# Rounding and halving the memory's weight slabs one place earlier in the queues of ScalarE and VectorE

## The chip, the cores and the metric

One core of one Trainium2 chip runs the whole program. The metric is the device time of one execution in microseconds (us); the kernel before was run three times and the median is compared.

## What is computed

The reference is two transformer blocks, one after the other, on 512 tokens of width 1024. The change touches the second block only, which has two layers. In each layer the memory's 256 tokens are normalised and projected to keys and values, the layer's own mixing output is projected and added to x, and x attends to the memory:

```python
mix = jnp.concatenate([out_a, out_b, out_c], axis=-1) @ w_mix_out[l]
x = x + rms_norm_2(mix, mix_post_g[l])
h = rms_norm_2(x, mem_pre_g[l])
mem_n = rms_norm_2(mem, mem_kv_g[l])
...
q = (h @ w_q).reshape(b, s, X_HEADS, X_HEAD_DIM)
kv = (mem_n @ w_kv).reshape(b, m, 2, X_HEADS, X_HEAD_DIM)
k, v = kv[:, :, 0], kv[:, :, 1]
sc = jnp.einsum('bqhd,bkhd->bhqk', q, k).astype(jnp.float32) * (X_HEAD_DIM ** -0.5)
p = jax.nn.softmax(sc, axis=-1).astype(v.dtype)
o = jnp.einsum('bhqk,bkhd->bqhd', p, v).reshape(b, s, D_MODEL)
return o @ w_o
```

## The kernel before

All weights come as one stream of slabs of 16 blocks of 128 x 128 numbers (1 MB). A slab passes four hands. SyncE loads it into one of four places of `ring` (`Stream.feed`, L372 issues). ScalarE rounds it to the short float form into one of three places of `ring_hi` (`Stream.round`, L264). VectorE subtracts this from the slab and writes the rest, its lower half, back over it, `ring_lo` (`Stream.halve`, L271). TensorE multiplies in three parts, upper by upper, upper by lower, lower by upper (`Stream.mm`, L322). TensorE reports each slab that it has begun (`slab_begun`). SyncE may load slab g once slab g-3 is begun, and ScalarE may round slab g once slab g-2 is begun, since `ring_hi` holds three.

The order on each engine is written out by hand. `ws.round_to(act, s, ...)` in ScalarE's code and `ws.halve_to(dve, s, ...)` in VectorE's put the roundings and halvings of all slabs up to s at that place of the queue. An engine works its queue in order, so whatever stands ahead of a rounding delays it.

Two stages matter. `mix_and_memory` (L1891) first projects the mixing output. Then TensorE makes eight key tiles, `key_tile(0)` to `key_tile(7)`, of 24 matmuls each, two tiles to a slab, and from two more slabs half of the values, 24 matmuls to a slab. Beside this, for each of eight column tiles of x, ScalarE evicts a key tile (`key_out`, L2009), rounds the new h (`round_h`, L2019) and squares x (L2020), while VectorE scales the projection (`scaled`, L2075), splits h (`split_h`, L2086) and adds to x (`new_x`, L2081). `round_h(n)` waits for `new_x(n)`, and `split_h(n)` for `round_h(n)`. Between these stand the slabs: `first_k` to `first_k + 3` are the keys', `first_v = first_k + 4` and `first_k + 5` the values', `first_q = first_k + 6` the first query slab.

`memory_attention` (L952) makes the remaining queries and values beside 16 softmax steps u. `upto` sets how many weight blocks TensorE has done beside step u. The table `rounds` says behind which step which slab is rounded and halved: ScalarE reads it after the exponential of step u, VectorE after its part of step u. Slab `AT_VALUE // SLAB`, here V, and V+1 hold the values' second half, V+2 to V+4 query tiles, V+5 the next stage's first weights. The first query matmul of V+2 also waits for ScalarE's two evictions of the values (`values_out`, L1082), which free its bank.

Of the kernel before, what the change touches and what calls it, by code (L numbers as in the profile page):

```python
# [28 lines left out]
KT = D // P  # L29
# [21 lines left out]
SLAB = 16  # L51
# [55 lines left out]
AT_VALUE = B2_AT["mq"] + 7 * SLAB  # L107
# [30 lines left out]
def build_program(nc, stream, xT_in, ctxT_in, memT_in, pos_in, const_in, axial_in, par1_in, par2_in, out):  # L138
    stack = ExitStack()
    with stack:  # L140
# [48 lines left out]
        def con(name, n=P, at=0):  # L189
            at += CONST[name]  # L190
            if CONST[name] >= CONST["freq"]:
                at -= CONST["freq"] - CONST["levels"]
            return const[:, at:at + n]
# [181 lines left out]
        ws = Stream()  # L375
# [246 lines left out]
        def root_of_mean(act, dst, sums):  # L622

            nc.scalar.activation(dst, sums, ACT.Ln, bias=con("eps", 1), scale=1.0 / D)
            act.drain()
            return nc.scalar.activation(dst, dst, ACT.Exp, scale=-0.5)
# [325 lines left out]
        def memory_attention(name, q, k, v, x, out, work, squares, total, scale, column):  # L952
# [2 lines left out]

            HEADS, N = KT // 2, KT // 2 * TB
            upto = (11, 22, 32, 34, 38, 42, 48, 50, 54, 58, 64) + (64,) * (N - 9)
            rounds = {0: AT_VALUE // SLAB + 1, 1: AT_VALUE // SLAB + 2, 2: AT_VALUE // SLAB + 3, 4: AT_VALUE // SLAB + 4, 8: AT_VALUE // SLAB + 5}
            VALUES = 2 * KT
            probs, probsT, stat = work  # L960
            tile_done = Signal("tile_done", KT)
# [929 lines left out]
        def mix_and_memory(x, post, memT, mem_hi, mem_lo, mem_scale, k_out, v_out, h_gain, sub_gain, sync, first):  # L1891
# [5 lines left out]
            first_k, first_v, first_q = at_k // SLAB, at_v // SLAB, AT_QUERY // SLAB  # L1897
# [105 lines left out]
            def scalar(act):  # L2003
                def leave(n):
                    nc.scalar.activation(post.raw[:, n, :], bank[:, n, :], ACT.Copy).then_inc(y_left.sem, 1)

                def key_out(j):
                    act.wait_ge(k_done.sem, k_done.at(j + 1))
                    nc.scalar.activation(k_out(j), bank[:, k_banks[j], 0:MEM], ACT.Copy, scale=256 ** -0.5).then_inc(k_read.sem, 1)  # L2009

                def value_out():
                    act.wait_ge(v_done.sem, v_done.at(1))
                    for tb in range(2):
                        nc.scalar.activation(v_out(0, tb), bank[:, v_banks[tb], :], ACT.Copy)

                def round_h(n):
                    t = AHEAD[n]
                    act.wait_ge(added.sem, added.at(n + 1))
                    nc.scalar.activation(h_hi[:, t, :], xT[:, t, :], ACT.Identity, scale=h_gain(t)).then_inc(h_rounded.sem, 1)  # L2019
                    nc.scalar.activation(post.raw[:, t, :], xT[:, t, :], ACT.Square)  # L2020

                def upper(k):
                    if k >= REST:
                        act.wait_ge(sub_normed.sem, sub_normed.at(k - REST + 1))
                    nc.scalar.activation(x.hi[:, k, :], x.whole[:, k, :], ACT.Copy).then_inc(rounded.sem, 1)

                ws.round_to(act, at // SLAB, ws.limit)
                upper(0)
                upper(1)
                for g in range(2):  # L2030
                    nc.scalar.activation(post.squares[:, 2 + g, :], x.whole[:, REST + g, :], ACT.Square).then_inc(sub_squared.sem, 1)
                upper(2)
                upper(3)
                ws.round_second(act, at // SLAB + 1)
                upper(4)
                upper(5)
                sub_scale = post.scale, post.next_scale
                for g in range(2):
                    act.wait_ge(sub_summed.sem, sub_summed.at(g + 1))
                    nc.scalar.activation(sub_scale[g], bank[:, 6 + g, :], ACT.Ln, bias=con("eps", 1), scale=1.0 / 64)  # L2040
                act.drain()
                for g in range(2):
                    nc.scalar.activation(sub_scale[g], sub_scale[g], ACT.Exp, scale=-0.5).then_inc(sub_scaled.sem, 1)
                upper(6)
                upper(7)
                act.wait_ge(sync.loaded.sem, sync.loaded.at(16))
                for k in range(KT if first else 0):
                    nc.scalar.activation(mem_squares[:, k, :], memT[:, k, :], ACT.Square).then_inc(mem_squared.sem, 1)
                for n in range(KT):
                    ws.round_to(act, (at + n * KT + KT - 1) // SLAB + SLABS_AHEAD, ws.limit)  # L2050
                    post.square(act, n)
                    if n in LEFT:
                        leave(n)
                    if n == 3 and first:
                        act.wait_ge(mem_summed.sem, mem_summed.at(1))
                        root_of_mean(act, mem_scale, bank[:, 7, 0:MEM]).then_inc(mem_scaled.sem, 1)
                    if n == 4:
                        for k in range(KT):
                            act.wait_ge(mem_normed.sem, mem_normed.at(k + 1))
                            nc.scalar.activation(mem_hi[:, k, :], memT[:, k, :], ACT.Copy).then_inc(mem_rounded.sem, 1)  # L2060
                ws.round_second(act, first_k + 1)
                post.rms(act)
                for n in range(KT):
                    key_out(n)
                    round_h(n)
                    if n % 2:
                        ws.round_to(act, first_k + n // 2 + 2, ws.limit)
                ws.round_to(act, first_q, ws.limit)
                value_out()

            def vector(dve):
# [53 lines left out]
                ws.halve_to(dve, first_k + 1, ws.limit)  # L2125
                dve.wait_ge(post.scale_ready.sem, post.scale_ready.at(1))
                dve.wait_ge(y_left.sem, y_left.at(len(LEFT)))
                halves = {1: first_k + 2, 4: first_k + 3, 6: first_v}
                for n in range(KT + 1):
                    if n < KT:  # L2130
                        scaled(n)
# [6 lines left out]
                ws.halve_to(dve, first_q, ws.limit)  # L2138

            stage("mix_and_memory", tensor=tensor, scalar=scalar, vector=vector, sync=sync.issue)  # L2140

        def scan_branch(keys, gates, q, v, y, work):
# [1057 lines left out]
        def layer_body(l, post_before):  # L3200
# [319 lines left out]
            with ExitStack() as here:  # L3520
                k = tmp("mem_k", [P, KT, MEM], here)
                v = tmp("mem_v", [P, 2, 4, 256], here)
                memT = tmp("memT", [P, KT, MEM], here)
                mem_lo = same_place("mem_lo", "memT", [P, KT, MEM], F32R)
                mem_hi = tmp("mem_hi", [P, KT, MEM], here, F32R)
                mix_and_memory(Split(h_hi, mix_lo, mix), PostNorm(lambda n: p2("mix_post", 1, n), raw, squares2, scales2, by_pool=False, alone=True),
                               memT, mem_hi, mem_lo, mem_root[:, :], lambda j: k[:, j, :],
                               lambda half, tb: v[:, tb, 2 * half:2 * half + 2, :].rearrange("p h n -> p (h n)"),
                               lambda t: p2("mem_pre", 1, t), gain_sub, Memory(memT[:, :, :]), l == 0)
                memory_attention("memory", raw, k, v, (mem_hi, mem_lo), mix,  # L3530
                                 (squares2, tmp("probsT3", [P, 2, MEM], here), tmp("stat3", [P, 2, 3, 1], here)),
                                 raw, squares2[:, 3, :], scales2[:, 0, :], tmp("q_column", [P, TB], here)[:, :])
# [220 lines left out]
```

## Time and profile before

| | |
|---|---|
| three runs | 2912.34, 2914.49, 2921.7 us |
| span of the profiled execution | 2911.1 us (its own time is not listed apart) |
| TensorE matmul busy | 2798.7 us, 96% |
| VectorE busy | 1652.6 us, 57% |
| ScalarE busy | 1175.9 us, 40% |
| mean granted TensorE clock | 0.991 |
| mean DMA | 86 GB/s |

The span reaches from the first to the last instruction; the run's time also holds what lies around it. Busy matmul time counts overlapping matmuls once, so a gap in it is time in which no matmul runs. `mix_and_memory` and `memory_attention` appear twice, around 1490 and 2343 us.

### The profile page before, as it was taken

Reading aid. Unit: us, or ns where it says so; the run is one execution under the profiler, and the core shown is the slowest. Engines: PE = TensorE matmul, PEld = TensorE weight load, DVE = VectorE, ACT = ScalarE, POOL = GpSimd, SP = SyncE. Lnnn points to the kernel's source line nnn. Section 1 sums busy time; section 2 is a strip of 40 time slices with the busy share of each in tenths; the row PEclk is TensorE's granted clock in tenths of the full one; section 3 lists DMA queues with packets and bytes.
Section 4 is the critical chain, followed back from the end, with each engine's and each line's share of the span. In section 5 each row is a group of like instructions: output and inputs, shape, how many; then the busy total and the mean of one; then the engine's idle time right before and its main releaser. Section 6 shows DMA issues by size and latency. Waiting matters only on the chain. (4 is left out here: it accounts for less than half of the span.)

```text
span 2911.1 us, 35813 instructions
## 1 busy us (share of the span) xinstructions
PE 2798.7 (96%) x14670; PEld 2254.8 (77%) x14670; DVE 1652.6 (57%) x2314; ACT 1175.9 (40%) x1719; POOL 288.2 (10%) x249
## 2 busy tenths in 40 slices
PE   8998999999999999999999999999999999999998
PEld 4898866678778888786687878888776778788886
DVE  5666266665645443568763466653667653566643
ACT  3832444432243332435653343333425543443332
POOL 0110033400001110001200001100002101011100
PEclk9999999999999999999999999999999999999999
DMA  6200210045423223220032122232220132232231
GB/s 255 73 15 1 94 47 27 30 167 177 152 72 102 88 101 101 97 73 30 30 118 100 59 87 102 89 109 101 73 72 16 59 116 73 73 101 95 93 102 58
DMA packets 46004, 249.53 MB, mean 86 GB/s; under 512 B 5136, under 2 KB 7312, under 8 KB 19344
## 3 DMA queue, kind: packets, MB, share of 16 engines
q1 hardware_dynamic: 45840, 247.23, 24.7%
q8 instruction: 117, 1.92, 0.3%
q14 instruction: 47, 0.39, 0.0%
HBM read 245.11 MB, written 2.10 MB: 85 GB/s over the span
## 5 line engine op out<-in xcount | busy, mean ns | idle before, releaser
L271 DVE TENSOR_TENSOR ring_lo<-ring,ring_hi 128x2048 fp32r<-128x2048 f32 x199 | 456.9, 2298 | 544.1 <-ACT ring_hi L264 544.1
L322 PE MATMUL bank<-h_hi,ring_hi 128*128 128x512 f32 x1360 | 543.9, 400 | 8.3 <-DVE ring_lo L271 4.1
L264 ACT ACTIVATE ring_hi<-ring 128x2048 fp32r<-128x2048 f32 x199 | 379.3, 1908 | 380.5 <-PE bank L322 352.0
L322 PE MATMUL bank<-h_hi,ring_lo 128*128 128x512 f32 x1360 | 530.6, 390 | 0.0
L1658 PE MATMUL bank<-h_hi,ring_hi 128*128 128x512 f32 x960 | 374.3, 390 | 0.0
L1662 PE MATMUL bank<-h_hi,ring_lo 128*128 128x512 f32 x960 | 373.5, 389 | 0.0
L1661 PE MATMUL bank<-h_lo,ring_hi 128*128 128x512 f32 x960 | 373.4, 389 | 0.0
L322 PEld LDWEIGHTS bank<-h_hi,ring_hi 128*128 128x128 f32 x1360 | 255.8, 188 | 66.2 <-issue 10.1
L322 PEld LDWEIGHTS bank<-h_hi,ring_lo 128*128 128x128 f32 x1360 | 255.7, 188 | 54.5
L322 PE MATMUL bank<-h_lo,ring_hi 128*128 128x512 f32 x624 | 243.2, 390 | 0.0
L1658 PEld LDWEIGHTS bank<-h_hi,ring_hi 128*128 128x128 f32 x960 | 180.2, 188 | 37.9 <-issue 0.5
L1661 PEld LDWEIGHTS bank<-h_lo,ring_hi 128*128 128x128 f32 x960 | 180.2, 188 | 37.6 <-issue 0.5
L1662 PEld LDWEIGHTS bank<-h_hi,ring_lo 128*128 128x128 f32 x960 | 180.2, 188 | 37.4
L322 PE MATMUL bank<-gated_lo,ring_hi 128*128 128x512 f32 x528 | 205.4, 389 | 0.0
L1781 DVE SCALAR_TENSOR_TENSOR mix<-bank,par,mix 128x511 f32<-128x511 f32 x176 | 123.8, 745 | 68.4 <-ACT mix L1727 64.8
L322 PEld LDWEIGHTS bank<-h_lo,ring_hi 128*128 128x128 f32 x624 | 117.5, 188 | 25.8 <-issue 4.1
L1575 POOL TENSOR_TENSOR raw<-raw,stat 128x512 f32<-128x512 f32 x64 | 65.2, 1040 | 647.2 <-DVE stat L1525 647.2
L1727 ACT ACTIVATE mix<-bank,par 128x512 f32<-128x512 f32 x88 | 63.7, 774 | 142.9 <-DVE bank L1789 142.9
L322 PEld LDWEIGHTS bank<-gated_lo,ring_hi 128*128 128x128 f32 x528 | 99.1, 188 | 20.5
L322 PE MATMUL bank<-mix_lo,ring_hi 128*128 128x512 f32 x272 | 112.8, 415 | 0.0
L1781 DVE SCALAR_TENSOR_TENSOR conv<-bank,par,conv 128x511 f32<-128x511 f32 x88 | 61.9, 745 | 69.8 <-ACT conv L1727 68.2
L1825 POOL TENSOR_TENSOR gated<-mix 128x512 f32<-128x512 f32 x44 | 57.1, 1297 | 447.3 <-ACT mix L1732 447.3
(470 smaller groups left out, 4875.6 us busy)
## 6 DMA issues: line engine op xcount, KB each, us to landing
ring<-in_stream SPq DMA_DIRECT2D x199, 1024.0 KB, 4.9
mod_w<-in_stream SPq DMA_DIRECT2D x64, 256.0 KB, 3.6
ring<-in_stream SPq DMA_DIRECT2D x7, 512.0 KB, 4.5
ring<-in_stream SPq DMA_DIRECT2D x10, 256.0 KB, 4.0
h_spare<-in_stream SPq DMA_DIRECT2D x2, 1024.0 KB, 9.3
xT<-in_xT SPq DMA_DIRECT2D x2, 1024.0 KB, 17.9
xT<-in_xT SPq DMA_DIRECT2D x1, 2048.0 KB, 9.4
memT<-in_memT SPq DMA_DIRECT2D x2, 1024.0 KB, 5.1
```

Of the source, the lines that this page charges most:

```text
L264: nc.scalar.activation(self.slab_hi(slab + j), self.slab(slab + j), ACT.Copy).then_inc(slab_rounded, 1)
L271: nc.vector.tensor_tensor(lower, self.slab(slab + j), self.slab_hi(slab + j).bitcast(F32), ALU.subtract)\
L322: ins = nc.tensor.matmul(out, lhsT, rhs, start=start and w is w_hi and x is x_hi, stop=stop and w is w_lo)
L1575: nc.gpsimd.tensor_tensor(p, p, stat[:, u % 2, 2, g:g + 1].to_broadcast([P, T]), ALU.mult)\
L1658: first = nc.tensor.matmul(out_ap[s], w_hi, x_hi, start=k == 0, stop=False)
L1661: nc.tensor.matmul(out_ap[s], w_hi, x_lo, start=False, stop=False)
L1662: last = nc.tensor.matmul(out_ap[s], w_lo, x_hi, start=False, stop=k == KT - 1)
L1727: last = nc.scalar.activation(work[:, j % 2, s, :], out_ap[s], ACT.Identity, bias=conv_b(col), scale=conv_w(2 * FT + col))
L1781: last = nc.vector.scalar_tensor_tensor(w, out_ap[s][:, 1 - lo:T - lo], conv_w(col), w, ALU.mult, ALU.add)
L1825: nc.gpsimd.tensor_tensor(gated(n), work[:, j % 2, 0, :], work[:, j % 2, 1, :], ALU.mult)\
```

## The change

In `mix_and_memory` ScalarE rounds slab `first_k + 2` before the first `key_out`, and the following ones behind n = 1, 3 and 5 instead of 3, 5 and 7. VectorE's halving of `first_k + 2` stays behind n = 1; those of the next three slabs move to n = 3, 5 and 7. In `memory_attention` the table gives step 0 two slabs, V+1 and V+2, and step 1 slab V+3; step 2 has none.

```diff
-            rounds = {0: AT_VALUE // SLAB + 1, 1: AT_VALUE // SLAB + 2, 2: AT_VALUE // SLAB + 3, 4: AT_VALUE // SLAB + 4, 8: AT_VALUE // SLAB + 5}
+            rounds = {0: AT_VALUE // SLAB + 2, 1: AT_VALUE // SLAB + 3, 4: AT_VALUE // SLAB + 4, 8: AT_VALUE // SLAB + 5}
...
                 ws.round_second(act, first_k + 1)
                 post.rms(act)
+                ws.round_to(act, first_k + 2, ws.limit)
                 for n in range(KT):
                     key_out(n)
                     round_h(n)
-                    if n % 2:
-                        ws.round_to(act, first_k + n // 2 + 2, ws.limit)
+                    if n % 2 and n < KT - 1:
+                        ws.round_to(act, first_k + n // 2 + 3, ws.limit)
                 ws.round_to(act, first_q, ws.limit)
                 value_out()
...
-                halves = {1: first_k + 2, 4: first_k + 3, 6: first_v}
+                halves = {1: first_k + 2, 3: first_k + 3, 5: first_v, 7: first_v + 1}
```

ScalarE's queue in `mix_and_memory`, from the square root (L626) to slab `first_k + 2` (L264), before:

```order
L626 ACTIVATE scales<-scales 128x512
L2009 ACTIVATE mem_k<-bank 128x256
L2019 ACTIVATE h_hi<-xT,par 128x512
L2020 ACTIVATE raw<-xT 128x512
L2009 ACTIVATE mem_k<-bank 128x256
L2019 ACTIVATE h_hi<-xT,par 128x512
L2020 ACTIVATE raw<-xT 128x512
L264 ACTIVATE ring_hi<-ring 128x2048
```

And the same place now:

```order
L626 ACTIVATE scales<-scales 128x512
L264 ACTIVATE ring_hi<-ring 128x2048
L2009 ACTIVATE mem_k<-bank 128x256
L2019 ACTIVATE h_hi<-xT,par 128x512
L2020 ACTIVATE raw<-xT 128x512
L2009 ACTIVATE mem_k<-bank 128x256
L2019 ACTIVATE h_hi<-xT,par 128x512
L2020 ACTIVATE raw<-xT 128x512
L264 ACTIVATE ring_hi<-ring 128x2048
```

The rounding of `first_k + 2` has moved ahead of two column tiles, and its old place is taken by that of `first_k + 3`.

VectorE's queue in the same stage, from the halving of `first_k + 2` (the first L271) to that of `first_k + 3`, before:

```order
L271 TENSOR_TENSOR ring_lo<-ring,ring_hi 128x2048
L2075 SCALAR_TENSOR_TENSOR raw<-bank,par,scales 128x512
L2086 SCALAR_TENSOR_TENSOR h_lo<-xT,par,h_hi 128x512
L2081 TENSOR_TENSOR xT<-xT,raw 128x512
L2075 SCALAR_TENSOR_TENSOR raw<-bank,par,scales 128x512
L2086 SCALAR_TENSOR_TENSOR h_lo<-xT,par,h_hi 128x512
L2081 TENSOR_TENSOR xT<-xT,raw 128x512
L2075 SCALAR_TENSOR_TENSOR raw<-raw,par,scales 128x512
L2086 SCALAR_TENSOR_TENSOR h_lo<-xT,par,h_hi 128x512
L2081 TENSOR_TENSOR xT<-xT,raw 128x512
L271 TENSOR_TENSOR ring_lo<-ring,ring_hi 128x2048
```

And now, where these lines are numbered one higher:

```order
L271 TENSOR_TENSOR ring_lo<-ring,ring_hi 128x2048
L2076 SCALAR_TENSOR_TENSOR raw<-bank,par,scales 128x512
L2087 SCALAR_TENSOR_TENSOR h_lo<-xT,par,h_hi 128x512
L2082 TENSOR_TENSOR xT<-xT,raw 128x512
L2076 SCALAR_TENSOR_TENSOR raw<-bank,par,scales 128x512
L2087 SCALAR_TENSOR_TENSOR h_lo<-xT,par,h_hi 128x512
L2082 TENSOR_TENSOR xT<-xT,raw 128x512
L271 TENSOR_TENSOR ring_lo<-ring,ring_hi 128x2048
```

Two groups of three operations stand between the halvings now, where there were three; the next two halvings follow at the same distance.

ScalarE's queue in `memory_attention`, from the exponential of step 0 (the first L1089), before:

```order
L1089 ACTIVATE squares,stat<-bank,stat,q_column 128x256
L264 ACTIVATE ring_hi<-ring 128x2048
L1089 ACTIVATE squares,stat<-bank,stat,q_column 128x256
L264 ACTIVATE ring_hi<-ring 128x2048
L1082 ACTIVATE mem_v<-bank 128x512 x2
L1089 ACTIVATE squares,stat<-bank,stat,q_column 128x256
L264 ACTIVATE ring_hi<-ring 128x2048
L1076 ACTIVATE raw<-bank 128x512 x2
```

And now:

```order
L1089 ACTIVATE squares,stat<-bank,stat,q_column 128x256
L264 ACTIVATE ring_hi<-ring 128x2048 x2
L1089 ACTIVATE squares,stat<-bank,stat,q_column 128x256
L264 ACTIVATE ring_hi<-ring 128x2048
L1082 ACTIVATE mem_v<-bank 128x512 x2
L1089 ACTIVATE squares,stat<-bank,stat,q_column 128x256
L1076 ACTIVATE raw<-bank 128x512 x2
```

V+2 is rounded behind step 0 and V+3 behind step 1; VectorE's halvings move the same way.

## Rows read from the trace of the kernel before

**Rows 1.** The page, busy us, share of the span, instructions of each engine

```profile
PE 2798.7 (96%) x14670; PEld 2254.8 (77%) x14670; DVE 1652.6 (57%) x2314; ACT 1175.9 (40%) x1719; POOL 288.2 (10%) x249
```

**Rows 2.** TensorE's waits, whole span: waited-for us in total, times, longest

```profile
PE bank L322 <- DVE ring_lo L271: 14.5, 8, 3.5
```

**Rows 3.** Timeline of TensorE: start us, us, engine, line, operation [idle before <-releaser]

```profile
1501.66 0.28 PE L322 MATMUL bank<-mem_hi,ring_lo 128*128 128x256 f32 x1
1502.01 0.35 PE L322 MATMUL bank<-mem_hi,ring_hi 128*128 128x256 f32 x1
...
1507.71 0.28 PE L322 MATMUL bank<-mem_hi,ring_lo 128*128 128x256 f32 x1
1511.48 0.36 PE L322 MATMUL bank<-mem_hi,ring_hi 128*128 128x256 f32 x1 [3.50 <-DVE ring_lo L271]
...
1518.81 0.47 PE L322 MATMUL bank<-ring_hi,mem_hi 128*128 128x512 f32 x1
...
1524.13 0.39 PE L322 MATMUL bank<-ring_lo,mem_hi 128*128 128x512 f32 x1
1526.05 0.50 PE L322 MATMUL bank<-ring_hi,mem_hi 128*128 128x512 f32 x1 [1.54 <-DVE ring_lo L271]
```

**Rows 4.** Timeline of VectorE, 1484 to 1532 us

```profile
1495.04 0.68 DVE L2081 TENSOR_TENSOR xT<-xT,raw 128x512 f32<-128x512 f32 x1
1499.57 2.29 DVE L271 TENSOR_TENSOR ring_lo<-ring,ring_hi 128x2048 fp32r<-128x2048 f32 x1 [3.85 <-ACT ring_hi L264]
...
1509.05 2.29 DVE L271 TENSOR_TENSOR ring_lo<-ring,ring_hi 128x2048 fp32r<-128x2048 f32 x1 [0.97 <-ACT ring_hi L264]
```

**Rows 5.** Timeline of ScalarE, 1484 to 1532 us

```profile
1491.22 0.63 ACT L626 ACTIVATE scales<-scales 128x512 f32<-128x512 f32 x1
1493.34 0.38 ACT L2009 ACTIVATE mem_k<-bank 128x256 f32<-128x256 f32 x1 [1.48 <-PE bank L322]
...
1497.63 1.90 ACT L264 ACTIVATE ring_hi<-ring 128x2048 fp32r<-128x2048 f32 x1
...
1507.12 1.89 ACT L264 ACTIVATE ring_hi<-ring 128x2048 fp32r<-128x2048 f32 x1
```

**Rows 6.** Group of `round_h` by line, 1489 to 1533.2 us: busy, mean ns, idle

```profile
L2019 ACT ACTIVATE h_hi<-xT,par 128x512 fp32r<-128x512 f32 x8 | 5.7, 717 | 8.5 <-DVE xT L2081 8.5
```

**Rows 7.** SyncE's issues (timeline), and the page: KB each, median us to landing

```profile
1477.99 0.33 SPq L372 DMA_DIRECT2D ring<-in_stream  x1
1490.58 0.33 SPq L372 DMA_DIRECT2D ring<-in_stream  x1
1496.33 6.39 SPq L372 DMA_DIRECT2D ring<-in_stream  x2
...
ring<-in_stream SPq DMA_DIRECT2D x199, 1024.0 KB, 4.9
```

**Rows 8.** Stretches: length, busy us of engines, granted clock, DMA share, GB/s

```profile
1508.00:1511.40 3.40, 0.00 (x0) 0.00 (x0) 2.43 (x3) 2.68 (x5) 0.00 (x0) 1.00 0.00 0
...
1513.40:1514.40 1.00, 1.00 (x6) 1.00 (x6) 0.87 (x2) 1.00 (x2) 0.00 (x0) 0.50 0.69 229
```

**Rows 9.** Timelines of the second stage: ScalarE, VectorE, TensorE

```profile
1548.42 1.91 ACT L264 ACTIVATE ring_hi<-ring 128x2048 fp32r<-128x2048 f32 x1
1559.59 1.08 ACT L1082 ACTIVATE mem_v<-bank 128x512 f32<-128x512 f32 x2 [0.48 <-PE bank L322]
...
1555.95 0.42 DVE L1125 TENSOR_REDUCE stat<-bank 128x1 f32<-128x256 f32 x1 [3.30 <-PE bank L1023]
1559.14 2.29 DVE L271 TENSOR_TENSOR ring_lo<-ring,ring_hi 128x2048 fp32r<-128x2048 f32 x1 [1.64 <-ACT ring_hi L264]
...
1561.58 0.47 PE L322 MATMUL bank<-h_hi,ring_hi 128*128 128x512 f32 x1 [2.03 <-DVE ring_lo L271]
```

**Rows 10.** Stretches around another pause of TensorE, columns as in rows 8

```profile
1292.00:1294.00 2.00, 0.00 (x0) 0.00 (x0) 1.99 (x5) 0.53 (x2) 0.00 (x0) 1.00 0.00 0
1294.00:1296.00 2.00, 1.68 (x8) 1.72 (x9) 0.00 (x0) 0.00 (x0) 0.00 (x0) 0.59 0.01 4
```

## Prediction

> **What bounds the kernel now.** I read the page first: TensorE is busy for 2798.7 of 2911.1 us, every other engine far less [rows 1]. So a rearrangement on ScalarE and VectorE can only pay where TensorE stands still for them. The list of TensorE's waits names such a place: its matmuls wait eight times for a lower half written by VectorE, 14.5 us in total, the longest 3.5 us [rows 2]. The timeline of TensorE shows where they lie, in layer 0 of the two layers. Write k for the first slab of memory keys, so that k+4 and k+5 hold the values' first half and k+6 is the first query slab.
>
> Inside a key tile matmuls start every 0.12 us, inside a value tile every 0.23 us. Against these, the starts leave a hole of 0.35 us ahead of slab k+2 (1502.01), 3.77 us ahead of k+3 (1511.48) and 1.92 us ahead of k+5 (1526.05) [rows 3]. I count the other four waits as the same places of layer 1, since both layers run the same queues and 14.5 us is twice what stands ahead of these slabs.
>
> Is the lower half really what ends the long hole? VectorE starts halving k+3 at 1509.05 and takes 2.29 us, to 1511.34; the matmul follows 0.14 us later [rows 4]. And VectorE itself came 0.97 us before for ScalarE's rounding, which began only at 1507.12 [rows 4, 5]. ScalarE rounds k+2 at 1497.63, although it sat idle for 1.48 us from 1491.85, and VectorE then idles 3.85 us for it [rows 4, 5]. So the chain is late because its first member stands late in a queue, not because an engine is full.
>
> **The change part by part.** No instruction is added or removed, and the queues of TensorE, GpSimd and SyncE are the same row by row. What moves, in each of the two layers, is four roundings of 1.90 us on ScalarE and three halvings of 2.29 us on VectorE in the first stage [rows 4, 5], and two of each in the second.
>
> *First stage, slab k+2.* Its rounding moves to right behind the square root, which ends at 1491.85. It needs slab k begun, which SyncE's next issue at 1490.58 shows, and its own data, issued at 1477.99 with a median of 4.9 us to landing [rows 5, 7]. So it runs 1491.8 to 1493.7. The first key tile's eviction moves from 1493.34 to 1493.6 [rows 5], 0.2 us later, and no more, because the idle 1.5 us ahead of it take in most of the 1.9. The second key tile is done 24 x 0.12 = 2.9 us later, by when ScalarE has caught up (0.72 us of `round_h` [rows 6] and a square in between): I take the 0.2 us as hidden there; without that room it would sit on every later tile. VectorE reaches its halving behind the addition at 1495.04 (0.69 us) plus the 0.2 us, at 1495.8 instead of 1499.57 [rows 4]: the lower half is there at 1498.1, 3.7 us ahead of TensorE.
>
> *The slabs behind it.* I carry this on with the spacing that before shows. Between the halving that ends at 1501.86 and the place of the next at 1508.08 (1509.05 less 0.97 idle) stand three groups of three VectorE operations, 2.1 us each [rows 4]. The new queue has two groups between halvings, so its period is 2 x 2.1 + 2.2 = 6.4 us. Halvings then start at 1495.8, 1502.1, 1508.4 and 1514.7 and end 2.3 us later. TensorE, unhindered, needs 48 x 0.12 = 5.8 us for a key slab and 24 x 0.227 = 5.45 us for a value slab, thus k+3 at 1507.7, k+4 at 1513.5, k+5 at 1519.0. The margins are 3.3, 2.8 and 2.0 us: they shrink, but stay positive to the end. ScalarE's roundings for these come at about 1497.6, 1503.5 and 1509.7, each over before VectorE asks. Loads: k+4 is issued at 1496.33, k+5 6 us after it, when k+2 begins [rows 7], so their data is there at about 1501 and 1507. k+6 is rounded at 1516 and halved by 1520.3, before the stage's matmuls end at 1524.4.
>
> Saved per layer: 3.77 - 0.12 = 3.65 us ahead of k+3; 1.92 - 0.23 = 1.7 us ahead of k+5; 0.35 - 0.12 = 0.2 us ahead of k+2.
>
> *The clock.* The long hole costs more than itself. In the 3.4 us from 1508.00 TensorE does nothing, its granted clock is still 1.00; from 1513.40 to 1514.40 it is 0.50, that is 1.2 instead of 2.4 GHz [rows 8]. The 48 matmuls of slab k+3 take 1518.81 - 1511.48 = 7.33 us, those of slab k+2 (1507.71 + 0.12) - 1502.01 = 5.82 us [rows 3]. With the hole gone I expect the fall gone: 1.5 us more per layer. The shorter holes, 1.92 us among them, are followed by no fall. The bounds are 0 and 1.5 us; I take 1.5, since nothing else in the stage idles TensorE for long.
>
> *Second stage.* ScalarE rounds two slabs, not one, behind the first exponential (1548.42); the second of them is the query slab V+2 (V is the first slab of values computed here). ScalarE is done with both at 1552.2, VectorE halves the first from about 1550.4 and the second to about 1554.9, ahead of VectorE's reduction at 1555.95 [rows 9], so no softmax step is delayed. Before, TensorE waits for V+2's half until 1561.58 (1559.14 + 2.29 = 1561.43) [rows 9]. What is late next: the same matmul needs the bank that ScalarE's two value evictions free, from 1559.59 for 1.08 us, to 1560.67 [rows 9]. So only 0.8 us of the 2.42 us between starts is won. V+3's rounding takes the old place of V+2's, ends 0.5 us ahead of these evictions and costs nothing while they wait for TensorE anyway. The 1.64 us rounding-to-halving idles on VectorE cost nothing either: it is not the bound there.
>
> The sum: 3.65 + 1.7 + 0.2 + 1.5 + 0.8 = 7.85 us per layer, 15.7 us for two. The profiled execution's own time is not listed apart from its span of 2911.1 us; the fastest run is 2912.34 and the median 2914.49, 3.4 us over the span. A saving inside the span passes one to one: span 2895.4, median 2914.49 - 15.7 = 2898.8 us. That is 0.54%; what a measurement of this kernel can tell from no change is about 0.3%, 8.7 us.
>
> **The rivals.**
>
> A, *the clock's fall moves instead of vanishing*. For it: falls elsewhere follow TensorE pauses no longer than these: after 1292 to 1294, empty, the clock is 0.59 in the next 2 us [rows 10]. Behind the change everything stands 8 and 16 us earlier, so another pause might be met or missed. Against: two layers show the fall at the same hole, and it goes with the longest one. A fall is worth 1.5 us by the two slabs above. With one more per layer than I count, the time is 2898.8 + 3.0 = 2901.8 us. The Trainium skill (TensorE: Matmul & The Clock Gate, Part 1: The HAM clock gate) says that activity is judged in windows that run freely and are not tied to the kernel's start, so where a fall lands varies from run to run. By that rule the 2 x 1.5 us is not certain to be gained, and as many may be gained or lost elsewhere; the trace agrees only in that pauses of similar length are treated differently.
>
> B, *the wait goes on to the next slab*. VectorE's operations wait for ScalarE's upper halves of h and these for VectorE's sums: over the eight tiles ScalarE idles 8.5 us for them [rows 6]. If these turns stretch the period from 6.4 us by more than 1 us, the three margins are eaten and TensorE waits at k+5. At before's own distance of 9.5 us between halvings (1499.57 to 1509.05) the half for k+5 would come at 1495.8 + 3 x 9.5 + 2.3 = 1526.6, where it comes now. Only the fall of the clock would be saved, and the 0.8 us, some 2.3 us per layer: 2914.5 - 4.6 = 2909.9 us. Midway, 2905. Against: that 9.5 us held three groups and an idle stretch that the change removes.
>
> C, *slower: ScalarE stands at a rounding with the evictions behind it*. Slab k+4's rounding waits for TensorE to begin k+2. It is reached at 1503.5 and k+2 begins at 1502.0, so it passes with 1.5 us to spare. If k+2 began later, the key evictions and upper halves behind it would stand too, and with them VectorE's chain, round after round. It decides from 1.5 us of lateness; to be slower than before it would have to eat 7.85 us and more per layer, with 12 us of added delay per layer for a time of 2914.5 + 8.3 = 2922.8. Nothing in the trace shows k+2 anything but early.
>
> D, *the change does not do what it says*. The instruction order leaves little room: the rounding stands first behind the root. Only a rounding held by its load would be the old one in a new place, and the load is issued 14 us ahead [rows 7]. I give it nothing of its own.
>
> **How the numbers follow.** Forecast 0.66 (2896 to 2901), A 0.18 (to 2902), B 0.14 (2905 to 2910), C 0.02. The median of three runs lies in a band of 2912.3 to 2921.7, so I add some 3 us to the low side and take in B's middle: 2893 to 2907. Faster by over 0.3% (below 2905.8): all of the forecast and A and a quarter of B, 0.87; within 0.3%: the rest of B, 0.11; slower 0.02.
>
> **What would show it.** In TensorE's list the waits for lower halves fall from 14.5 us and eight to under 1 us and some two. No pause of over 0.4 us between the key matmuls; the clock is 1.00 throughout the stage; from slab k+2's first matmul to k+5's the time falls from 24.0 us (1526.05 less 1502.01) to 17.2. VectorE halves four slabs 6.4 us apart, the first some 4 us behind the square root. In the second stage the first V+2 matmul follows the evictions, not a halving, 1.6 us between starts. I am wrong if a wait for a lower half of over 1 us stands at k+4 or k+5 (B), or if the waits are gone but the time is not (A, or a wait elsewhere).

## The result and the profile after

| | before | changed |
|---|---|---|
| median of the runs | 2913.86 us (6 runs, 2911.89 to 2921.87) | 2900.84 us (6 runs, 2892.47 to 2904.76) |
| ratio to before, 95% interval | | 0.9948 [0.9931, 0.9966] |
| profiled execution: time, span | span 2911.1 us | 2904.76, span 2902.9 us |
| mean granted clock of that execution | 0.991 | 0.989 |

The change makes the kernel 0.52% faster, 13.0 us between the medians. The profiled execution of the changed kernel is the slowest of its six. One of the later executions of the kernel before, beside the experiments, took 6104 us, twice as long as any other, and enters no ratio.

The page's line on the engines is that of [rows 1] but for TensorE: its matmuls are busy for 5.3 us more and its weight loads for 2.3 us more, every other engine within 0.5 us:

```profile
PE 2804.0 (97%) x14670; PEld 2257.1 (78%) x14670; DVE 1652.7 (57%) x2314; ACT 1176.4 (41%) x1719; POOL 288.0 (10%) x249
```

TensorE's waits, the line that stood at 14.5 us and eight times in [rows 2]:

```profile
PE bank L322 <- DVE ring_lo L271: 0.3, 2, 0.2
```

The two that are left are those of 0.16 us at slab V+1. ScalarE's timeline in the first stage of layer 0, to be held against [rows 5] (start us, us, line, operation, idle before):

```profile
1498.40 0.63 ACT L626 ACTIVATE scales<-scales 128x512 f32<-128x512 f32 x1
1498.94 1.90 ACT L264 ACTIVATE ring_hi<-ring 128x2048 fp32r<-128x2048 f32 x1
1500.74 0.36 ACT L2009 ACTIVATE mem_k<-bank 128x256 f32<-128x256 f32 x1
...
1503.39 0.38 ACT L2009 ACTIVATE mem_k<-bank 128x256 f32<-128x256 f32 x1 [1.16 <-PE bank L322]
...
1504.81 1.90 ACT L264 ACTIVATE ring_hi<-ring 128x2048 fp32r<-128x2048 f32 x1
```

The rounding of k+2 fills the idle time behind the root. The first eviction comes 2.34 us behind the root's start instead of 2.12, and by the second ScalarE waits for TensorE again, 1.16 us where it was 1.36 before: the 0.2 us are absorbed. VectorE's halvings in the same stretch, against [rows 4]:

```profile
1503.02 2.29 DVE L271 TENSOR_TENSOR ring_lo<-ring,ring_hi 128x2048 fp32r<-128x2048 f32 x1
...
1509.29 2.28 DVE L271 TENSOR_TENSOR ring_lo<-ring,ring_hi 128x2048 fp32r<-128x2048 f32 x1
...
1515.57 2.29 DVE L271 TENSOR_TENSOR ring_lo<-ring,ring_hi 128x2048 fp32r<-128x2048 f32 x1
...
1521.85 2.28 DVE L271 TENSOR_TENSOR ring_lo<-ring,ring_hi 128x2048 fp32r<-128x2048 f32 x1
```

None of the four has an idle time in brackets: VectorE finds each upper half ready. They lie 6.3 us apart. TensorE begins the slabs k+2, k+3, k+4 and k+5, and then the second stage, at these places (timeline; against [rows 3]; PEq is TensorE's own sequencer):

```profile
1508.95 0.28 PE L322 MATMUL bank<-mem_hi,ring_hi 128*128 128x256 f32 x1
...
1514.71 0.28 PE L322 MATMUL bank<-mem_hi,ring_hi 128*128 128x256 f32 x1
...
1520.47 0.40 PE L322 MATMUL bank<-ring_hi,mem_hi 128*128 128x512 f32 x1
...
1525.94 0.39 PE L322 MATMUL bank<-ring_hi,mem_hi 128*128 128x512 f32 x1
...
1532.96 0.47 PE L322 MATMUL bank<-h_hi,ring_hi 128*128 128x512 f32 x1 [1.42 <-PEq L380]
```

The halves end at 1511.57, 1517.86 and 1524.13, so they lead by 3.1, 2.6 and 1.8 us. The stretches of this stage show TensorE without a pause and its clock without a fall (columns as in rows 8):

```profile
1509.00:1515.00 6.00, 6.00 (x52) 6.00 (x52) 5.87 (x8) 4.92 (x8) 0.00 (x0) 1.00 0.49 176
1515.00:1520.00 5.00, 5.00 (x44) 5.00 (x44) 5.00 (x7) 3.80 (x6) 0.00 (x0) 1.00 0.65 206
1520.00:1526.00 6.00, 6.00 (x31) 5.04 (x30) 5.61 (x6) 4.39 (x6) 0.00 (x0) 1.00 0.54 180
```

From the first key matmul (1497.05, before 1489.86) to the second stage's first (1532.96, before 1533.20) it is 35.91 us instead of 43.34, in layer 1 the same: 7.43 us per layer. In the second stage, against [rows 9]:

```profile
1559.33 1.09 ACT L1082 ACTIVATE mem_v<-bank 128x512 f32<-128x512 f32 x2 [0.48 <-PE bank L322]
...
1560.46 0.50 PE L322 MATMUL bank<-h_hi,ring_hi 128*128 128x512 f32 x1 [1.18 <-ACT mem_v L1082]
```

The matmul before this one starts at 1558.90, so 1.56 us lie between starts instead of 2.42, and what ends the wait is now the eviction. That is 0.86 us per layer. Together 2 x 8.29 = 16.6 us are gone from the two places, but the spans differ by 8.2 us and the medians by 13.0. The experiments also ask where the rest went.

### The profile page after: what moved, and what is told of

The parts are those of the page before. It is cut to its first block and busy times, and to the rows that moved or that the text cites. A ratio compares the mean times of both kernels' runs of the same rounds, so it can differ in the third digit from the quotient of the medians.

```text
span 2902.9 us, 35813 instructions
## 1 busy us (share of the span) xinstructions
PE 2804.0 (97%) x14670; PEld 2257.1 (78%) x14670; DVE 1652.7 (57%) x2314; ACT 1176.4 (41%) x1719; POOL 288.0 (10%) x249
## 5 line engine op out<-in xcount | busy, mean ns | idle before, releaser
L271 DVE TENSOR_TENSOR ring_lo<-ring,ring_hi 128x2048 fp32r<-128x2048 f32 x199 | 456.9, 2298 | 526.3 <-ACT ring_hi L264 526.3
L322 PE MATMUL bank<-h_hi,ring_hi 128*128 128x512 f32 x1360 | 544.6, 400 | 6.2 <-PEq L380 3.9
L264 ACT ACTIVATE ring_hi<-ring 128x2048 fp32r<-128x2048 f32 x199 | 379.3, 1908 | 382.3 <-PE bank L322 351.3
L322 PE MATMUL bank<-h_hi,ring_lo 128*128 128x512 f32 x1360 | 531.2, 391 | 0.0
L322 PEld LDWEIGHTS bank<-h_hi,ring_hi 128*128 128x128 f32 x1360 | 256.4, 189 | 64.2 <-issue 10.4
L322 PEld LDWEIGHTS bank<-h_hi,ring_lo 128*128 128x128 f32 x1360 | 255.9, 188 | 54.7
L322 PE MATMUL bank<-h_lo,ring_hi 128*128 128x512 f32 x624 | 243.3, 390 | 0.0
L322 PE MATMUL bank<-gated_lo,ring_hi 128*128 128x512 f32 x528 | 205.4, 389 | 0.0
L322 PEld LDWEIGHTS bank<-h_lo,ring_hi 128*128 128x128 f32 x624 | 117.6, 188 | 25.9 <-issue 4.1
L322 PEld LDWEIGHTS bank<-gated_lo,ring_hi 128*128 128x128 f32 x528 | 99.1, 188 | 20.8
L322 PE MATMUL bank<-mix_lo,ring_hi 128*128 128x512 f32 x272 | 113.9, 419 | 0.0
```

What stands on the lines that cost most here:

```text
L264: nc.scalar.activation(self.slab_hi(slab + j), self.slab(slab + j), ACT.Copy).then_inc(slab_rounded, 1)
L271: nc.vector.tensor_tensor(lower, self.slab(slab + j), self.slab_hi(slab + j).bitcast(F32), ALU.subtract)\
L322: ins = nc.tensor.matmul(out, lhsT, rhs, start=start and w is w_hi and x is x_hi, stop=stop and w is w_lo)
```

## The experiments

In what follows, "first stage" is the time from the first key matmul to the second stage's first matmul, read from TensorE's timeline; times are medians, the ratios are to the kernel before run beside them. Theory: the late rounding of k+2 and of the slabs behind it on ScalarE was the cause. Rivals: VectorE's order carried a part; the second stage did; one early rounding is enough. The changed kernel itself was run beside them only once more, for its second profile.

**One stage alone.** The changed kernel with the old table, and the old kernel with the new table:

```diff
-            rounds = {0: AT_VALUE // SLAB + 2, 1: AT_VALUE // SLAB + 3, 4: AT_VALUE // SLAB + 4, 8: AT_VALUE // SLAB + 5}
+            rounds = {0: AT_VALUE // SLAB + 1, 1: AT_VALUE // SLAB + 2, 2: AT_VALUE // SLAB + 3, 4: AT_VALUE // SLAB + 4, 8: AT_VALUE // SLAB + 5}
```

> Only the first stage is changed; the table of the second stage is as before. My theory: nearly all of the gain is here. From the first key matmul to the first matmul of the second stage 35.9 us instead of 43.3, in both layers; in the second stage the 2.42 us between starts ahead of slab V+2 come back. Time: 2 x 7.4 = 14.9 us below before, so about 2899, ratio 0.995. Rival (the second stage's earlier roundings matter beyond their own wait): the time stands 4 us or more above that of the whole change at the same clock.

> Only the table of the second stage is changed. My theory: 1.56 us between starts ahead of V+2 instead of 2.42, ended by ScalarE's value evictions, and 43.3 us in the first stage as before, with the clock's fall there. Time: 2 x 0.86 = 1.7 us below before, ratio 0.999, which timing can't tell from 1. Rival (the table alone removes more, because two roundings leave step 2): 4 us or more.

The first gave 2903.41 us, ratio 0.9953 [0.9938, 0.9967], first stage 35.92 us in both layers, V+2's gap 2.42. The second gave 2912.41, 0.9991 [0.9981, 1.0], which can't be told from no change, first stage 43.38 and 43.35, V+2's gap 1.56. So the places behave as expected and independently: 7.4 us and 0.86 us per layer. In time the first stage alone lies 10.4 us below before rather than 14.9, so the time falls short of the places here too. It lies 2.6 us above the whole change; at the same mean granted clock, 0.990, three of its runs took 2903.2 to 2903.8 us and the one of the whole change 2903.39. That is not the 4 us that the rival asked for.

**One engine alone.** The first stage's change (old table) with VectorE's halvings at their old places, and the old kernel with only the halvings moved:

```diff
-                halves = {1: first_k + 2, 3: first_k + 3, 5: first_v, 7: first_v + 1}
+                halves = {1: first_k + 2, 4: first_k + 3, 6: first_v}
```

> First stage with ScalarE's roundings moved, VectorE's halvings at the old places (1, 4, 6, end). My theory: the late rounding was the whole cause, VectorE's order hardly matters. With 2.1 us per group the halves of k+3, k+4 and k+5 are ready 0.9, 0.2 and 0.5 us before TensorE wants them, so the first stage takes 35.9 us, at most 0.5 more, and the time is that of the first stage's change, ratio 0.995. Rival (the halvings' new places carry a good part): a wait for a lower half of over 1 us at k+3 or k+4, first stage 37 us or more.

> First stage with VectorE's halvings moved to 3, 5 and 7, ScalarE's roundings at the old places. My theory: VectorE then stands at each halving for a rounding that itself stands behind VectorE's later sums, so the chain gets longer: k+3's half comes when it came before, k+4's about 2 us too late and k+5's about 4 us too late for TensorE. First stage about 48 us instead of 43.3 in both layers, time 9 us above before, ratio 1.003. Rival (moving either side helps): first stage below 43 us.

ScalarE alone: 2903.99 us, 0.9948 [0.9928, 0.9969], first stage 35.92 and 35.98 us, no wait for a lower half at k+3 to k+5. The halvings in VectorE's timeline:

```profile
1500.20 2.28 DVE L271 TENSOR_TENSOR ring_lo<-ring,ring_hi 128x2048 fp32r<-128x2048 f32 x1
...
1508.64 2.29 DVE L271 TENSOR_TENSOR ring_lo<-ring,ring_hi 128x2048 fp32r<-128x2048 f32 x1
...
1514.91 2.29 DVE L271 TENSOR_TENSOR ring_lo<-ring,ring_hi 128x2048 fp32r<-128x2048 f32 x1
...
1520.59 4.49 DVE L271 TENSOR_TENSOR ring_lo<-ring,ring_hi 128x2048 fp32r<-128x2048 f32 x2
```

They come 8.4, 6.3 and 5.7 us apart, none after an idle. The halves of k+3, k+4 and k+5 are ready 1.0, 0.5 and 0.25 us before TensorE's first matmul with them (1511.90, 1517.66 and 1523.13), where the whole change has 3.1, 2.6 and 1.8. The stage is as long as with the first stage's whole change: the halvings' new places bring nothing that can be seen but their larger lead.

VectorE alone: 2929.67 us, 1.0043 [1.0029, 1.0057], first stage 49.22 and 49.26 us. Half of the change is slower than none. Its halvings:

```profile
1503.75 2.29 DVE L271 TENSOR_TENSOR ring_lo<-ring,ring_hi 128x2048 fp32r<-128x2048 f32 x1 [3.85 <-ACT ring_hi L264]
...
1513.22 2.29 DVE L271 TENSOR_TENSOR ring_lo<-ring,ring_hi 128x2048 fp32r<-128x2048 f32 x1 [3.11 <-ACT ring_hi L264]
...
1522.70 2.29 DVE L271 TENSOR_TENSOR ring_lo<-ring,ring_hi 128x2048 fp32r<-128x2048 f32 x1 [3.11 <-ACT ring_hi L264]
...
1532.18 2.29 DVE L271 TENSOR_TENSOR ring_lo<-ring,ring_hi 128x2048 fp32r<-128x2048 f32 x1 [3.11 <-ACT ring_hi L264]
```

VectorE reaches the first halving 3.85 us and each later one 3.11 us before the upper half is there, and ScalarE meanwhile has work whose input stands behind that halving. Each round of this takes 9.5 us. I had expected 48 us: the size was 1.2 us short, the way right. The median is 15.8 us above before where I had expected 9; the longer first stage in two layers makes 11.8 of it, and this profile has the most time at the lower clock of all, 71.7 us before TensorE's work ends.

**One slab alone.** The old kernel with the rounding of k+2 behind the square root and all else at the old places:

```diff
                 post.rms(act)
+                ws.round_to(act, first_k + 2, ws.limit)
```

> The kernel before with one rounding moved, that of slab k+2 to behind the square root; all other roundings and halvings of both stages at their old places. My theory: each slab's rounding has its own part. k+2 is early, k+3's half comes just in time, k+4's about 1.6 us late and k+5's about 2 us late, because their roundings stand behind the upper halves of h of tiles 5 and 7. First stage about 39.6 us, half of the gain; time about 7.5 us below before, ratio 0.9975. Rival (one early start is enough, the chain keeps its lead): first stage 36 us, no wait for a lower half of over 0.5 us.

First stage 39.63 us in both layers. TensorE's waits in it, layer 0:

```profile
1518.16 0.47 PE L322 MATMUL bank<-ring_hi,mem_hi 128*128 128x512 f32 x1 [1.34 <-DVE ring_lo L271]
...
1525.41 0.50 PE L322 MATMUL bank<-ring_hi,mem_hi 128*128 128x512 f32 x1 [1.54 <-DVE ring_lo L271]
```

These are the beginnings of k+4 and k+5, 1.62 and 1.93 us behind the matmul before. Half of the gain belongs to the first rounding and half to those behind it, as expected. But the time is 2911.99 us, 0.9992 [0.9983, 1.0001], 1.3 us below before where the two stages give 7.4 and where I had expected 7.5. All ten runs lie between 2909.5 and 2914.4 us, so the loss is not the scatter of one run.

**Is the clock's fall on the path?** The long hole filled with work for TensorE in the old kernel:

```diff
+                    if j == 6:
+                        keep_busy(pe, 14, k_banks[j])
                     for k in range(KT):
```

> The kernel before, with 14 idle-filling 128x128 matmuls ahead of key tile 6, about 3.2 us of work in the 3.8 us hole (they overwrite a bank that the tile starts afresh). They keep TensorE busy, so its granted clock should stay 1.00 and slab k+3's 48 matmuls take 5.8 us instead of 7.3. My theory after the first four runs: the last halving, not TensorE, sets the stage's end, so the clock's fall was hidden: the gap ahead of k+5 grows from 1.92 to 3.4 us and the stage stays 43.3 us, time as before, ratio 1.000. Rival (my prediction's own reading, 1.5 us per fall on the path): the stage takes 41.8 us, time 3 us lower, ratio 0.999, gap ahead of k+5 stays 1.9 us.

The result is 2913.8 us, 0.9996 [0.9985, 1.0008], first stage 43.39 and 43.38. The hole is filled and the clock stays at 1.00, as two stretches show (columns as in rows 8):

```profile
1511.60:1515.00 3.40, 3.17 (x29) 2.98 (x27) 2.43 (x3) 2.74 (x5) 0.00 (x0) 1.00 0.02 5
1515.00:1522.00 7.00, 6.01 (x48) 5.80 (x48) 5.90 (x7) 4.72 (x7) 0.00 (x0) 1.00 0.45 150
```

TensorE's waits after it:

```profile
1515.05 0.38 PE L322 MATMUL bank<-mem_hi,ring_hi 128*128 128x256 f32 x1 [0.28 <-DVE ring_lo L271]
...
1522.47 0.47 PE L322 MATMUL bank<-ring_hi,mem_hi 128*128 128x512 f32 x1 [1.42 <-DVE ring_lo L271]
...
1529.72 0.50 PE L322 MATMUL bank<-ring_hi,mem_hi 128*128 128x512 f32 x1 [1.52 <-DVE ring_lo L271]
```

Slab k+3 takes 5.8 us instead of 7.3, and a wait of 1.42 us appears ahead of k+4, where there had been none. So the fall cost nothing in the old kernel: TensorE at full speed would have waited for the half of k+4 instead. The mean granted clock of these runs is 0.992 at the median, against 0.991, and the time is the same. The wait came one slab earlier than I had written; the stage's length is as expected, and the rival with 41.8 us falls.

**Where the missing time went.** Both kernels once more, unchanged, for second profiles:

> The kernel before, unchanged, for a second profile. My theory: the clock falls at other places than in the first profile, ahead of 1490 us too, and the first key matmul of layer 0 stands some us off 1489.86; the first stage still takes 43.3 us and V+2's gap 2.42. Rival (the places of the falls belong to the kernel, so that the changed one has more): the same falls as in the first profile, first key matmul at 1489.9 within 0.5 us.

> The changed kernel, unchanged, for a second profile. My theory: first stage 35.9 us and V+2's gap 1.56 us in both layers again, while the first key matmul of layer 0 stands elsewhere than 1497.05 by some us, between 1489 and 1499, with the number of clock falls ahead of it. Rival: 1497.0 within 0.5 us.

Before: 2911.63 us, span 2909.8, first key matmul at 1488.69, first stage 43.34, V+2's gap 2.41. Changed: 2897.38 us, span 2895.6, first key matmul at 1492.78, first stage 35.92, gap 1.56. The stages repeat to 0.02 us, what lies around them does not. The first key matmul of layer 0 stands ahead of every changed instruction, yet in the ten changed profiles (two of the changed kernel, eight of variants, all with the same program up to there) it lies between 1488.64 and 1497.05 us. In the first pair of profiles it is 7.2 us later in the changed kernel, which is most of the 8.4 us by which the spans miss the 16.6.

Each trace holds a record of the granted clock, either 1.00 or 0.50. Summed up over the time before the first key matmul and over all time until TensorE's work ends, the stretches at 0.50 are:

| profile | first key matmul | at 0.50 before it | at 0.50 in all |
|---|---|---|---|
| before | 1489.86 us | 23.9 us | 41.0 us |
| before, again | 1488.69 us | 23.9 us | 41.0 us |
| changed, again | 1492.78 us | 30.7 us | 37.5 us |
| one slab alone | 1492.92 us | 30.7 us | 51.2 us |
| changed | 1497.05 us | 41.0 us | 54.6 us |

The later the first key matmul, the more time was spent at 0.50 ahead of it; among all twelve profiles those with the same sum differ by up to 1.2 us. In the kernel before, both profiles have the same ten falls, nine of them 1.3 us earlier in the second and one 2.1 us later. I had expected other places, so as to the falls the rival was right for this kernel. The changed kernel's two profiles differ: falls near 395 and 624 us stand in the first alone, falls near 298 and 516 us in the second alone.

What does a fall cost where TensorE is the bound? From the first matmul of V+2 to the 24th of line L322 behind it, it takes 7.5 us in the kernel before and 9.1 us in the one-slab kernel, which has a fall of 3.4 us there, in both layers: 1.6 us, about half of the fall's length. Taken at half their length, and the 6.8 us of the kernel before that lie behind the long holes at nothing, the falls cost 17 us in the kernel before and 27 in the changed one. The difference of 10 us stands against the 8.4 that are missing between the spans. In the second pair it is 1.6 us against 2.4. In the one-slab kernel, whose span is that of the kernel before to 0.1 us, it is 8.5 against 7.4. So the falls account for the missing time to within 2 us each time. This is an account read from the traces; no run forced the falls to other places. The run times go with the clock too: of the executions whose mean granted clock was 0.991, the kernel before took 2911.5 to 2913.5 us in all 25 (beside the experiments), the changed one 2898.2 and 2898.3 in its two, 14 us less.

Inside the second stage a pause of the same length is followed by a fall in one kernel and not in the other. Stretches before, in and behind V+2's gap (2.41 us between starts) there:

```profile
1558.20:1560.90 2.70, 0.70 (x4) 0.24 (x3) 2.29 (x1) 1.34 (x3) 0.00 (x0) 0.99 0.00 0
1560.90:1564.00 3.10, 3.08 (x7) 2.47 (x8) 0.00 (x0) 0.00 (x0) 0.00 (x0) 0.50 0.37 98
```

And in the kernel before, around the same gap of 2.42 us:

```profile
1559.50:1561.50 2.00, 0.05 (x1) 0.00 (x0) 1.93 (x1) 1.08 (x2) 0.00 (x0) 1.00 0.00 0
1561.60:1565.00 3.40, 3.40 (x15) 2.85 (x16) 0.00 (x0) 0.00 (x0) 0.00 (x0) 1.00 0.58 178
```

Seven broad matmuls in 3.1 us against fifteen in 3.4: the same pause is followed by 1.2 GHz in one and by 2.4 GHz in the other. The one-slab kernel has this fall in both layers, the first stage's change with the old table has it in both too, the kernel before in neither, in either of its profiles. ScalarE's part alone has it in layer 0 and not in layer 1, 2.41 and 2.42 us between starts ahead of these stretches:

```profile
1558.50:1564.00 5.50, 5.50 (x17) 4.39 (x18) 0.00 (x0) 0.00 (x0) 0.00 (x0) 0.69 0.59 191
2406.50:2412.00 5.50, 5.50 (x27) 4.63 (x28) 0.26 (x1) 0.00 (x0) 0.00 (x0) 1.00 0.55 194
```

So what an earlier stage saves can be taken back by a later pause that now meets a fall. That is shown for this place. What makes a pause meet one stays open, and with it why most of the old kernel's runs crowd near 2912 to 2914 us, with some up to 2922, while the changed kernel's spread from 2892 to 2905; I tried nothing that would move a fall by itself.

**A version that beats both.** With the wait passed to the evictions, these are next. First, V+2's tile waits only for the eviction of its own bank:

```diff
-                        if n == 2:
-                            pe.wait_ge(values_read.sem, values_read.at(2))
+                        if n < 4:
+                            pe.wait_ge(values_read.sem, values_read.at(n - 1))
```

> The changed kernel; in the second stage the V+2 query tile waits only for the first value eviction, whose bank it takes, and the next tile for the second. My theory: the wait ahead of V+2 now ends with the first of two evictions, 0.5 us earlier: 1.0 to 1.1 us between starts instead of 1.56. Time 1 us below the whole change's, about 2900, ratio to before 0.994. Rival: ScalarE's reading beside TensorE's writing of the neighbouring bank costs it back, or the wait passes to V+2's lower half: 1.5 us between starts.

It gave 2897.37 us, 0.9939 [0.9921, 0.9958], and V+2's gap 1.08 us in both layers:

```profile
1557.03 0.50 PE L322 MATMUL bank<-h_hi,ring_hi 128*128 128x512 f32 x1 [0.69 <-ACT mem_v L1082]
```

ScalarE reads one bank beside TensorE's writing of the other at no cost that can be seen: the two evictions take 1.09 us as before. The gap gives 1.0 us in two layers; the median lies 3.5 us below that of the changed kernel, which was not run beside it, so 2.5 us of that are not shown to be the edit's. Then the order of the second value slab, in both stages, with the evictions split to match:

```diff
-                            value_block(*divmod(done[0], 2))
+                            if done[0] < KT:
+                                value_block(*divmod(done[0], 2))
+                            else:
+                                value_block(KT // 2 + done[0] % (KT // 2), done[0] // (KT // 2) - 2)
...
+                        if last_values:
+                            values_out(0)
                         if u in rounds:
                             ws.round_to(act, rounds[u], ws.limit)
+                        if last_values:
+                            values_out(1)
...
-                    for k in range(KT):
-                        for tb in range(2):
+                    for k, tb in [divmod(i, 2) for i in range(KT)] + [(half + i % half, i // half) for i in range(KT)]:
```

> A try to beat both kernels: the changed kernel with the previous run's separate waits for the two value evictions, and in both stages the second value slab's matmuls finish the first 128 memory tokens before they begin the second, so that ScalarE evicts one bank while TensorE fills the other; in the second stage the first eviction stands ahead of the rounding of V+3. My theory: ahead of V+2 the starts lie 0.3 to 0.6 us apart instead of 1.56, and from the last value matmul to the second stage 1.3 us instead of 1.8, since one eviction (0.6 us) is left at the end instead of two (1.08). Saved against the change: 1.6 us per layer, 3.2 in all, about 2897, ratio to before 0.993. Rival (V+2's matmul then waits for something else, its lower half or the softmax): starts stay 1 us or more apart.

It gave 2892.9 us, 0.9928 [0.9915, 0.9942], with the first stage at 35.43 us and V+2's matmul 0.22 us behind the one before: no gap is left, less than the 0.3 to 0.6 us that I had expected. The stage's end:

```profile
1524.07 0.47 PE L322 MATMUL bank<-h_hi,ring_hi 128*128 128x512 f32 x1 [0.93 <-PEq L380]
```

That is 1.31 us behind the last value matmul instead of 1.81. Against the whole change it saves 1.34 us at V+2 and 0.48 us in the first stage, 3.6 us for two layers, and the median is 7.9 us lower, though the two were not run beside each other. The 4 us beyond that are of the size by which the falls of the clock vary (27.3 us at 0.50 in this kernel's profile, 37.5 and 54.6 in the changed one's); I count 3.6 us as shown.

## Why the prediction was right

The predicted time was 2898.8 us with a range of 2893 to 2907; 2900.84 was measured. The forecast's saving of 15.7 us stands against 16.6 in the places that the change touches and 13.0 between the medians. That the median came within 2.0 us is partly luck: the places gave 0.9 us more than the sum, and the falls elsewhere, which the sum has at nothing, took some 3.6 back. The step "a saving inside the span passes one to one" did not hold: of 16.6 us 8.2 passed in one pair of profiles and 14.2 in the other, and in the one-slab kernel nothing of 7.4.

*What bounded the kernel.* The reading that the chain was late through its first member's place in ScalarE's queue held: ScalarE's part alone brings the first stage to 35.92 us, VectorE's alone makes it 49.2.

*The count of the waits.* The prediction took all eight waits for lower halves as those ahead of k+2, k+3 and k+5 in two layers. That was misread. In each layer the four are those at k+3 (3.50), k+5 (1.54), V+2 (2.03) and V+1 (0.16 us), 7.2 us together; the 0.35 us ahead of k+2 are not in the list. The sum did not suffer, since it prices V+2 by itself.

*The schedule.* Halvings 6.4 us apart, 3.3, 2.8 and 2.0 us of lead: measured 6.3 us and 3.1, 2.6 and 1.8. From k+2's to k+5's first matmul 17.2 us were said, 16.99 measured. The three terms of that stretch (3.65, 1.7 and 1.5) make 6.85, measured 7.05 (24.04 less 16.99), and the 0.2 ahead of k+2 was 0.25. Another 0.13 us lie behind k+5's first matmul, where I had counted none.

*The clock's term.* This step was wrong in its reading, though not in its sum. I priced the fall at 1.5 us on the path, with 0 as the other bound. The filled hole shows that it cost nothing by itself, since the half of k+4 was ready only 0.15 us before the slowed TensorE asked for it (VectorE began it at 1516.37 in the profile before: 1516.37 + 2.29 = 1518.66, against 1518.81 in [rows 3]). The 1.5 us are rightly in the sum only because the whole chain of halves moved: TensorE's timeline counts them as slow matmuls, and without the fall they would have been a wait. Rival A took its price of 1.5 us per fall from the same place, where the fall was free. For falls where TensorE is the bound it is nearly right all the same: 1.6 us at V+2.

*The second stage.* 0.8 us were predicted, 0.86 measured, with the evictions as the next thing late. No softmax step is delayed: against the stage's first matmul the exponentials of steps 0 and 1 keep their places, and that of step 2 comes 0.8 us earlier, with V+2.

*The rivals.* A, falls of the clock elsewhere, is what parts 16.6 from 13.0 us as far as the traces tell: I priced it at 3.0 us and gave it 0.18, and in a form of it, it happened. The fall at the long hole did not move, it went; more falls came at other pauses. The Trainium skill (TensorE: Matmul & The Clock Gate, Part 1: The HAM clock gate) says that the window in which activity is judged doesn't begin anew with a kernel, so that the point at which the clock changes varies. The trace agrees where a pause of 2.4 us ahead of V+2 is followed by a fall in one layer and not in the other of the same execution, and where the changed kernel's two profiles differ in their falls; the kernel before, with the same ten falls in both of its profiles, shows no such variation. B did not occur in the changed kernel. The kernel with VectorE's part alone shows the turns between ScalarE and VectorE that B feared: halvings 9.5 us apart, the distance that I had priced it by. C did not occur: no rounding of the stage has an idle before it, and that of k+4 is reached at 1510.57, 1.6 us after k+2 is begun. D did not either.

## What to carry to other kernels

When a chain of producers feeds the bound engine, look for the first one that stands behind other work in its queue while it had idle time earlier; move that one, and check by the spacing of the rows how long the lead lasts over the slabs behind it. Move a consumer's step only behind its producer's: halving earlier without rounding earlier cost 0.43% here. Do not add up a pause and the slow clock behind it as two costs before asking what TensorE would have waited for at full speed, and read what a change of some microseconds does from the stage's own length in the trace. What is left of it in the whole run is a second question, which the falls of the clock elsewhere decide: here 7.4 us in the stages left 1.3 in the median.

## What the runs showed of the hardware

Three things I had not expected. A fall of the granted clock to 0.50 can be free: 48 matmuls took 7.3 instead of 5.8 us and the stage's length was 43.3 us either way. Where TensorE was the bound, at V+2, a fall of 3.4 us cost 1.6 us. Pauses of one length are not treated alike: of the pauses of 2.4 us ahead of V+2, in seven profiles and two layers each, seven were followed by a fall and seven were not. The same kernel text ahead of the change came to the first key matmul anywhere between 1488.64 and 1497.05 us in twelve profiles, with 23.9 to 41.0 us at the lower clock ahead of it, and 7.4 us saved in the two stages of the one-slab kernel showed as 1.3 us in its median.
